# A scheduled eight-core decoder step: longer DMA times in its planner, one more weight buffer for the second stream, an earlier rank for the norms, and the first weight fetch gated on the second row block

## The reference, cut to what matters

```python
for l in range(DEPTH):                      # DEPTH = 2
    hp = _rms(xp, norm_mix[l])
    if l % 2 == 0:                          # layer 0: attention + gated MLP chunks
        q, k, v, zu, zv = _ab_project(hp, w_in_ab[j], q_norm[j], k_norm[j])
        a = _swa_prompt(q, k, v, rel_bias, attn_sink[j])
        b, gv = _chunk_gmlp(zu, zv, ...)
        xp = xp + jnp.concatenate([a, b], axis=-1) @ w_out_ab[j]
    else:                                   # layer 1: HGRN2 recurrence
        o, s = _hgrn_mixer(hp, w_in_c[j], lb[l], c_out_norm[j], w_out_c[j], s0)
        xp = xp + o
    xp = xp + (silu(h @ w_gate[l]) * (h @ w_up[l])) @ w_down[l]   # h = _rms(xp, norm_ffn[l])
```

## Time and profile before

| | us |
|---|---|
| median of three runs | 1672.18 |
| the profiled execution | 1671.38 |
| its span on the slowest core (core 2) | 1669.8 |
| span of the eight cores | 1641.0 to 1669.8 |
| PE busy on core 2 | 1576.3 (94%) |
| DVE, ACT, POOL busy | 997.5, 624.5, 456.4 |
| chain that ended last | PE 82%, DMA 9%, issue 3% |

### The profile page before, as it was taken

The page is one execution under the profiler, slowest core; times in us unless marked ns, Lnnn a source line. Parts: engine busy times, 40 slices in busy tenths (PEclk is TensorE's granted clock), DMA queues, the critical chain, the costliest instruction groups (busy, mean ns, idle before and its releaser), DMA issues.

```text
span 1669.8 us, 35006 instructions; the slowest of 8 cores (1641.0 to 1669.8 us)
## 1 busy us (share of the span) xinstructions
PE 1576.3 (94%) x11690; PEld 979.4 (59%) x11831; DVE 997.5 (60%) x2111; ACT 624.5 (37%) x1173; POOL 456.4 (27%) x778
## 2 busy tenths in 40 slices
PE   4899999999999999989998999998998999999998
PEld 2455446766656765556564767566554468676443
DVE  4775645765557776546544665478677567654332
ACT  2754424544226643234312332254441256422100
POOL 3452122212222223321313322234344222122110
PEclk9999999999999999989999999999999999999999
DMA  9689799969959989987698758689998756355541
GB/s 202 143 137 161 132 174 179 165 106 173 177 109 192 160 156 182 187 198 195 180 205 229 137 106 174 128 171 191 187 186 198 161 135 135 114 169 189 169 159 73
DMA packets 76526, 272.36 MB, mean 163 GB/s; under 512 B 8656, under 2 KB 10352, under 8 KB 76320
## 3 DMA queue, kind: packets, MB, share of 16 engines
q0 software_dynamic: 56800, 204.50, 65.6%
q1 hardware_dynamic: 13120, 47.74, 8.2%
q10 hardware_dynamic: 6432, 17.88, 3.1%
HBM read 374.36 MB, written 44.60 MB: 251 GB/s over the span
## 4 chain that ended last, share of the span: by engine, by line
PE 82%; DMA 9%; issue 3%; DVE 2%; ACT 2%; POOL 1%; SPq 0%; ACTq 0%; DVEq 0%; POOLq 0%
PE bank L1057 35%; PE bank L1077 17%; PE bank L782 10%; PE bank L1117 6%; DMA X<-xin 3%; PE bank L1148 3%; PE bank L1199 3%; DMA X<-sin 2%; PE bank L773 1%; PE bank L931 1%; DMA sts<-X 1%; DMA y<-X 1%; PE bank L996 1%; POOL st L661 1%; DMA wt<-cvt 1%
## 5 line engine op out<-in xcount | busy, mean ns | idle before, releaser
L1057 PE MATMUL bank<-hT,wt 128*128 128x264 bf16 (+3 forms) x4188 | 672.5, 315 | 9.7 <-DVE hT L776 5.5
L1057 PEld LDWEIGHTS bank<-hT,wt 128*128 128x128 bf16 x4224 | 409.5, 98 | 226.4 <-issue 13.8
L648 POOL DMA_DIRECT2D wt<-wall x284 | 160.3, 566 | 643.9 <-PE bank L1057 199.9
L1077 PE MATMUL bank<-wt,af 128*128 128x512 bf16 x1411 | 317.1, 379 | 7.2 <-issue 3.0
L1061 ACT ACTIVATE ft<-bank 128x320 f32<-128x320 f32 (+3 forms) x264 | 122.3, 464 | 414.3 <-PE bank L1057 398.1
L1062 DVE SCALAR_TENSOR_TENSOR ft<-ft,bank 128x320 f32<-128x320 f32 (+3 forms) x264 | 136.9, 521 | 199.3 <-ACT ft L1061 198.3
L1077 PEld LDWEIGHTS bank<-wt,af 128*128 128x128 bf16 x1452 | 139.7, 98 | 165.9 <-issue 5.6
L1083 DVE SCALAR_TENSOR_TENSOR X<-bank,X 128x512 f32<-128x512 f32 (+1 forms) x140 | 93.1, 666 | 144.1 <-PE bank L1077 138.2
L1063 DVE TENSOR_TENSOR af<-ft,bank 128x320 bf16<-128x320 f32 (+3 forms) x264 | 137.4, 521 | 58.1 <-PE bank L1057 42.6
L661 POOL TENSOR_TENSOR st<-st,mhalf 128x1 f32<-128x1 f32 (+5 forms) x153 | 130.8, 855 | 20.6 <-DVE st L832 0.4
L1117 PE MATMUL bank<-wt,hT 128*128 128x256 bf16 x1056 | 129.1, 278 | 2.4 <-DVE hT L776 2.4
(11 more groups left out here) (213 smaller groups left out, 1702.9 us busy)
## 6 DMA issues: line engine op xcount, KB each, us to landing
wt<-wall POOLq DMA_DIRECT2D x260, 512.0 KB, 9.7
wt<-wsc POOLq DMA_DIRECT2D x104, 512.0 KB, 5.8
wsc<-wt SPq DMA_DIRECT2D x44, 512.0 KB, 9.0
X<-xin SPq DMA_DIRECT2D x18, 512.0 KB, 10.9
wt<-wall POOLq DMA_DIRECT2D x24, 384.0 KB, 7.8
y<-X ACTq DMA_DIRECT2D x16, 512.0 KB, 5.5
X<-sin SPq DMA_DIRECT2D x16, 512.0 KB, 8.5
sts<-X ACTq DMA_DIRECT2D x16, 512.0 KB, 8.5
```

What stands on the lines that cost most here:

```text
L648: S.op("pool", lambda e: e.dma_start(out=b.ap[:, 0:cols], in_=wall[g][:, 0:cols]), w=[b], dma=b, nbytes=512 * cols, lead=lead, prio=prio)
L1057: i = e.matmul(b.ap[:, 0:n], lhsT=w.ap[:, o + k * 128:o + k * 128 + 128], rhs=hT[st.par][:, k, lo:lo + n], start=(k == 0), stop=(k == 7))
L1077: i = e.matmul(b.ap[0:n], lhsT=act[k].ap[:, st.sl(blk)], rhs=w[k // 4].ap[:, (k % 4) * 512:(k % 4) * 512 + 512], start=(k == 0), stop=(k = ...
```

## The change

Five edits. (1) A planner-wide `lead` is added to that of every operation; inside `norm` it is 0.06 of a phase, elsewhere 0. (2) In the plan a DMA of SP or ACT begins 4.5 us after its issue (2.0 before) and counts as landed 2.5 us after its end (1.2 before); one of POOL 5.0 us (3.5) and 1.7 us (1.2). (3) Stream 1 may hold 8 weight buffers (7 before). (4) The gate of q0 on X0 is gone. (5) kv, the first weight tile, waits for the landing of X1. No operation is added or removed; the order on each engine is planned anew.

```diff
+        self.lead = 0.0
...
-        o.fn, o.dma, o.nbytes, o.lead, o.prio = fn, dma, nbytes, lead, prio
+        o.fn, o.dma, o.nbytes, o.lead, o.prio = fn, dma, nbytes, lead + self.lead, prio
...
-                d0, w = max(t + (3.5 if e == "pool" else 2.0), ring[e]), o.nbytes / DMA_BW
+                d0, w = max(t + (5.0 if e == "pool" else 4.5), ring[e]), o.nbytes / DMA_BW
...
-                o.fin = ring[e] + 1.2
+                o.fin = ring[e] + (1.7 if e == "pool" else 2.5)
...
-        pW = mkpool("wt", 10, 2048, BF16, dma=True, fifo=True, margin=0.4, caps={0: 7, 1: 7})
+        pW = mkpool("wt", 10, 2048, BF16, dma=True, fifo=True, margin=0.4, caps={0: 7, 1: 8})
...
+        NLEAD = 0.06
...
         def norm(st, bl, gain):
+            S.lead = NLEAD
+            norm_blocks(st, bl, gain)
+            S.lead = 0.0
+
+        def norm_blocks(st, bl, gain):
...
-        early["q0"].writer.deps.add(X[0].writer)
+        early["kv"].writer.deps.add(X[1].writer)
```

## The result

| | before | after |
|---|---|---|
| median of five runs, us | 1671.01 (1667.30 to 1674.11) | 1653.56 |
| profiled execution / its span | 1671.38 / 1669.8 | 1653.56 / 1652.0 |
| spans of the eight cores | 1641.0 to 1669.8 | 1639.1 to 1652.0 |
| PE busy on the slowest core | 1576.3 (94%) | 1585.9 (96%) |

The ratio of after to before is 0.9877, with a 95% interval of 0.9845 to 0.9908: 1671 x 0.0123 = 20.6 us faster, and 17.5 us by the medians. The prediction was 1649.0 us, 23 us faster.

A forecast was written before the change was run, and what follows sets the result against it. The prediction took the slowest core to be bound by transfers later than planned. Start -6, DMA times -19 and -3, lead 0, eighth buffer 0, new order +5 gave -23 us, so 1649 us; range 1632 to 1680.

The forecast's parts named there:

- The sum: Whole kernel: start, DMA times, lead, eighth buffer and new order added together give -23 us, for 1649 us; chance 0.58.
- What bounds it: Slowest core: the plan believes transfers faster than they are; late-transfer stalls and lower clock make the 28.8 us spread.
- The DMA times, -19 and -3: Planned SP and ACT transfers 3.8 us longer: -19 us from late-transfer stalls, -3 from the stall at phase 4's end.
- none over 2 us at L1298: Sign expected in the new profile: no PE stall over 2 us at the state loads of line L1298.
- The start, -6: First 40 us: with kv held back, X blocks land earlier and the q matmuls start about 6 us sooner.
- the third rival: No net effect: new order eats the landings' gain, the start is taken back before phase 1; 1672 us, chance 0.10.
- The lead, 0: Ends of phases 2 and 5: lead leaves PE's hT waits of 1.87 and 3.06 us; 0, bounds -5 and +5.
- The eighth buffer, 0: Weight buffers of stream 1: nothing on PE waits for weights, so an eighth gains 0 us.
- the slower rival: Phases with both streams: eighth buffer starves stream 0, 34 us of weight waits; 1683 us, chance 0.15.
- The new order, +5: All engine lists: the new order brings stalls the plan doesn't see, +5 us, bounds 0 and +15.
- Only the start: Rival: plan moves consumers but finds nothing to put before them, only the start gains; 1666 us, chance 0.17.

The follow-up runs named there:

- e7: Before with the new DMA times alone: ratio to before 1.0140, clock hold included; slowest span 1681.5 us, 1655.8 less the time lost at clock 0.81.
- e8: Before with the new gate alone (kv waits for X1): ratio to before 0.9993, slowest span 1676.0 us.
- e1: After with the old gate (q0 waits for X0, kv for nothing): ratio to before 0.9961; slowest span 1657.9 us less the time lost at clock 0.81.
- e2: After with the old DMA times in the plan: ratio to before 1.0027; slowest span 1674.7 us less the time lost at clock 0.81.
- e9: After unchanged, run again on chip C: ratio to before 0.9863, slowest span 1651.5 us.
- e4: After with 7 weight buffers for stream 1 instead of 8: ratio to before 0.9901; slowest span 1651.5 us less the time lost at clock 0.81.
- e3: After with a norm lead of 0 instead of 0.06: ratio to before 0.9949; slowest span 1652.2 us less the time lost at clock 0.81.
- e12: After with POOL's two DMA times at their old values, SP's and ACT's new: ratio to before 0.9899, slowest span 1656.9 us.
- e6: After with a norm lead of 0.05 instead of 0.06: ratio to before 1.0063; slowest span 1701.6 us, 1650.7 less the time lost at clock 0.81.
- e5: After unchanged, run again on chip B: median 1683.07 us, no ratio; slowest span 1681.3 us, 1652.8 less the time lost at clock 0.81.
- e10: After with the two table loads waiting for q1 instead of u1: ratio to before 0.9881; slowest span 1659.3 us less the time lost at clock 0.81.
- e11: After with the two table loads waiting for u0 and ahead of the wsT load: ratio to before 0.9896, slowest span 1652.4 us.

## Why the prediction was right, and where it wasn't

**The sum.** -23 us predicted, -17.5 (medians) to -20.6 (ratio) measured. The kind of cause and the largest term were right. That the rest of the sum came out too is in part luck, as the starts of phase 1 show (first feed-forward matmul, us, mean of cores 0 to 3):

| | old DMA times | new DMA times |
|---|---|---|
| old gate | 111.3 (before) | 116.4 (e7) |
| new gate | 107.5 (e8) | 106.6 (after) |

The new times cost phase 0 5.1 us, which no term of the sum had. The gate wins 3.8 us there with the old times, but 9.8 with the new ones, and so pays for that cost as well (after has the lead and the eighth buffer too; against e1, at 115.3, the gate wins 8.7).

- *What bounds it.* Right. With the old times (before, e2, e8) the spread of the cores and the stalls behind late transfers are there together, with the new ones (after, e9) both are small. Clock is a smaller part of the gain than of the spread: below full clock the slowest core lost 21.7 us before and about 17 after, 5 of the 17.8 us that it gained. The slowest clock came out at 0.990, not above it.
- *The DMA times, -19 and -3.* Right in kind, and in size as far as these runs tell. Taking the edit out of after costs 23.4 us on the slowest core (21 by the ratios to e4), adding it alone to before brings 14.0 (16 by the dies without a hold), with the cost in phase 0 in it, and -22 was predicted. Two thirds of the stalls was a fair share: after still has the state load of 4.15 us. The claim "none over 2 us at L1298" was wrong on that core: this is a store followed by a load, 11.01 + 15.80 us on the chain, well above the added 7.6 us of cover plus what the plan had.
- *The start, -6.* Right in total, by parts that miss in both directions. X1's landing and kv's issue came as worked out (8.4 for 8.3 and 9.07 for 9 us), X4's square at 15.9 where I had 21, the q run at 25.8 where I had 28.0. The rate of 4.7 us per block was read from a stretch with the weight queue running; with kv issued only at 9, X2 to X4 seem to have had a freer path than that. But that the gain at the start passes on, whatever the other edits do, was the unchecked step. Taken out of after, the gate is 4.7 to 6.6 us. Alone on before it is 0: more than half is given back in phase 0, as the third rival had it, and longer waits at the late blocks go with the loss of the rest (e8). The terms of the sum were not independent, and the sum didn't say so.
- *The lead, 0.* The size was nearly right (0.9 to 2.7 us), the mechanism wrong. "The lead doesn't move them" rested on due times alone, 2.85 for the down blocks and 2.94 for the next norm. The rows of after show a norm block's transposes ahead of the last down matmuls all the same, and both waits shrank (e3 and after), by 4.2 us together, inside the bound of -5 that I gave. Why the planner put them there isn't shown.
- *The eighth buffer, 0.* Right; e4 is within 0.4 us, and the slower rival with its 34 us of weight waits is refuted. The one weight wait that came (3.50 us on the slowest core, up to 6 in other runs) stays with the cap at 7. I had written that a weight wait would speak for this rival; it goes with the new times for SP and ACT instead (it is in e12, and not in e2).
- *The new order, +5.* The sum, which ended at -23, would have been -28 without it. The order has its own stalls: the weight wait of 3.50 us, 3.13 at 701.90, 1.97 and 2.55 in phase 0. It isn't to be separated from the rest by these runs. Two orders that differ by a lead of 0.01 are 0.6 us apart, corrected (e6). One cost that belongs to this term is shown, the 5.1 us in phase 0 above.
- *Only the start.* Refuted: with the new times the stalls at the value row and near 900 us are gone, so the plan did find other work.

## What to carry to other kernels

When all cores execute the same lists and their times spread, look at the slow ones' long stalls for late transfers, and give a planner the landing times of the loaded kernel, not those of a free ring: it was the edit that carried this change. An edit that wins time ahead of such a wait can be worth nothing until the wait is mended (the gate: 0 alone, about 6 us with the new times), so a sum of separate gains needs the order in which they are to be had. And measure a gain of one per cent on more than one chip: here it was 1.2 and 1.4% on two, and on a third, where the clock falls, nothing.

## What was not expected of the hardware

In some runs TensorE's granted clock stays at 0.81 for a stretch, with the engine at full work. Windows of e5, core 2 (columns as in the earlier trace rows):

```profile
60.00:86.00 26.00, 21.11 (x167) 11.93 (x170) 20.77 (x57) 18.84 (x27) 12.08 (x25) 0.87 0.53 88
88.00:246.00 158.00, 156.56 (x789) 74.53 (x803) 76.73 (x171) 50.65 (x90) 39.51 (x63) 0.81 0.77 128
252.00:290.00 38.00, 37.71 (x194) 17.98 (x197) 18.09 (x25) 9.11 (x14) 8.73 (x18) 1.00 0.85 163
```

and core 0 of the same execution:

```profile
88.00:246.00 158.00, 157.93 (x946) 79.58 (x944) 91.78 (x190) 58.29 (x101) 46.38 (x77) 1.00 0.91 149
```

In the same 158 us core 2 does 789 matmuls and core 0 946. 158 x 0.19 = 30 us, and the spans differ by 28.5. The length depends on the chip: about 155 to 162 us on chips B and C (e5, e6, e7, e10), 4 to 15 us on chip A, there several times per core, most often at about 90, 290, 510 and 660 us, 3.5 to 4.5 us on cores 0 to 3 in the profile of after, none in e9, e11 and e12. The profiles of before and e8 have none anywhere. Four of eight cores in e5 (2 to 5), all eight in e6, one die in e7, cores 0 and 1 in e10. (The expectations speak of 62 to 69 us for its begin; these were counted from the first record of the clock, which is some 23 us into the span.)

The stretch in e5 begins at about 86 us. Ahead of it, behind the stall of 2.55 us at 74.57 and among sparse matmuls, the clock was at half, its 1.2 GHz, as in this window of the same core:

```profile
76.00:80.00 4.00, 2.49 (x21) 1.96 (x21) 3.77 (x8) 4.00 (x6) 3.59 (x6) 0.50 0.01 2
```

The Trainium skill ("TensorE: Matmul & The Clock Gate", section "Seeing it yourself") knows a peak-current limit that takes a whole die to 13/16 of the clock when three of its cores run dense matmuls, and holds it while the load lasts. 13/16 is the 0.81 of these rows. Otherwise they differ: in e5 two cores of each die were held and the other two not, and core 2 came back to 1.00 at about 250 us with PE 99% busy (37.71 of 38 us). What sets a hold off, and why its length differs so between chips, stays open. I suspected the many cores that leave the sparse phase 0 at about the same time, now that they are in step, but e9 has the same lists and no hold.

The record does show which edit it goes with. On chip B every one of the 21 executions of e5, e6 and e7 has two or more cores with a mean clock of 0.978 or less. Of the 30 of before and e8, 21 have none, and these are all that count in their ratios. e7 differs from before by the new DMA times alone. And a stretch that begins between 83 and 100 us, near the end of phase 0, is in eight of the eleven profiles with the new times for SP and ACT (not in e9, e11 and e12, all on chip C), and in none of the three with the old ones (before, e2, e8). So on chip B the edit that takes the stalls away brings the hold with it; what in the new order does so isn't shown.

What it costs: on chip B it took all of the change's gain, and the profiles of e1, e3 and e4 on chip A hold 7 to 13 us of it on the slowest core. Not all of that is in their ratios, perhaps, since before, which has no profile on chip A, may have such stretches there too: the lowest clock among its cores is 0.981 there in the median, against 0.984 on chip B.
